# One sum on DVE and one multiply on PE for each statistic of the convolution branch's layer norm

## The reference

```
def layer_norm(x, g=None, b=None):
    mu = jnp.mean(x32, axis=-1, keepdims=True)
    var = jnp.mean(jnp.square(x32 - mu), axis=-1, keepdims=True)
    y = (x32 - mu) * lax.rsqrt(var + LN_EPS)
...
h_c = causal_dwconv(c_a * jax.nn.sigmoid(c_b), cf_w, cf_b)
y_c = jax.nn.silu(layer_norm(h_c, cf_ln_g, cf_ln_b)) * jax.nn.silu(c_g)
g_m = jax.nn.sigmoid(merge).reshape(bsz, slen, N_BRANCH, D_MODEL)
m = (g_m[:, :, 0] * (y_a @ w_branch[0])
     + g_m[:, :, 1] * (y_b @ w_branch[1])
     + g_m[:, :, 2] * (y_c @ w_branch[2]))
```

## Time and profile before

| | |
|---|---|
| median of 3 runs | 2294.22 us (2293.9 to 3189.31) |
| the profiled execution | 2294.44 us, span 2292.6 us |
| PE busy | 2214.4 us, 97% of the span |
| DVE busy | 1250.4 us, 55% |
| ACT busy | 779.0 us, 34% |
| mean granted TensorE clock | 0.986 |
| data moved | 217.93 MB, mean 95 GB/s |

### The profile page before, as it was taken

The page is one execution under the profiler, slowest core; times in us unless marked ns, Lnnn a source line. Parts: engine busy times, 40 slices in busy tenths (PEclk is TensorE's granted clock), DMA queues, the critical chain, the costliest instruction groups (busy, mean ns, idle before and its releaser), DMA issues.

```text
span 2292.6 us, 25818 instructions
## 1 busy us (share of the span) xinstructions
PE 2214.4 (97%) x10758; PEld 1822.4 (79%) x10770; DVE 1250.4 (55%) x1656; ACT 779.0 (34%) x1112; POOL 35.4 (2%) x46
## 2 busy tenths in 40 slices
PE   3999999999999799999999999999999999999998
PEld 2788888888788697877788888889787778888887
DVE  7798797933454836422745554224642375555422
ACT  1223232223343244344343333224434434333211
POOL 1000000000000110000000000000000000000000
PEclk7999999999999999999999999999999999999999
DMA  8332332332133222222123322213222222332221
GB/s 301 116 102 91 106 97 79 110 110 92 60 106 115 71 77 74 92 92 74 56 74 110 103 94 98 101 65 97 69 92 92 74 74 65 102 110 92 93 101 74
DMA packets 188242, 217.93 MB, mean 95 GB/s; under 512 B 3808, under 2 KB 167262, under 8 KB 188126
## 3 DMA queue, kind: packets, MB, share of 16 engines
q1 hardware_dynamic: 184128, 210.52, 27.7%
q10 hardware_dynamic: 3262, 3.60, 0.5%
q0 software_dynamic: 736, 2.15, 0.2%
HBM read 212.06 MB, written 4.19 MB: 94 GB/s over the span
## 4 chain that ended last, share of the span: by engine, by line
PE 91%; DVE 6%; ACT 1%; issue 1%; POOL 0%; DMA 0%; SPq 0%; ACTq 0%; POOLq 0%; DVEq 0%
PE psum L1582 28%; PE psum L1583 28%; PE psum L1584 28%; DVE whl L459 1%; PE psum L1807 1%; DVE adsum L1037 1%; PE psum L1796 1%; PE psum L1819 1%; PE psum L1878 1%; PE psum L1849 1%; PE psum L1860 1%; DMA x<-in_x 0%; DVE stat L1006 0%; PE psum L1906 0%; ACT whl L452 0%
## 5 line engine op out<-in xcount | busy, mean ns | idle before, releaser
L1582 PE MATMUL psum<-hT,whl 128*128 128x512 f32 (+1 forms) x2112 | 805.2, 381 | 8.5 <-DVE hT L1059 5.8
L1583 PE MATMUL psum<-hT,whl 128*128 128x512 f32 (+1 forms) x2112 | 797.3, 377 | 0.0
L1584 PE MATMUL psum<-hT,whl 128*128 128x512 f32 (+1 forms) x2112 | 797.2, 377 | 0.0
L459 DVE TENSOR_TENSOR whl<-raw,whl 128x1024 fp32r<-128x1024 f32 (+1 forms) x368 | 449.8, 1224 | 610.4 <-ACT whl L452 610.4
L452 ACT ACTIVATE whl<-raw 128x1024 fp32r<-128x1024 f32 (+1 forms) x368 | 384.4, 1048 | 478.0 <-PE psum L1584 441.3
L1582 PEld LDWEIGHTS psum<-hT,whl 128*128 128x128 f32 x2112 | 399.2, 189 | 90.9 <-DVE hT L1059 9.2
L1584 PEld LDWEIGHTS psum<-hT,whl 128*128 128x128 f32 x2112 | 399.2, 189 | 73.4
L1583 PEld LDWEIGHTS psum<-hT,whl 128*128 128x128 f32 x2112 | 399.5, 189 | 71.1 <-issue 0.7
L1582 PE MATMUL psum<-whl,ff 128*128 128x512 f32 x352 | 139.2, 396 | 2.2 <-DVE fsil L1561 2.2
L1584 PE MATMUL psum<-whl,ff 128*128 128x512 f32 x352 | 138.9, 395 | 0.0
L1583 PE MATMUL psum<-whl,ff 128*128 128x512 f32 x352 | 138.9, 395 | 0.0
(11 more groups left out here) (268 smaller groups left out, 2167.4 us busy)
## 6 DMA issues: line engine op xcount, KB each, us to landing
raw<-in_w_in SPq DMA_DIRECT2D x88, 1024.0 KB, 5.1
raw<-in_w_up SPq DMA_DIRECT2D x44, 1024.0 KB, 5.1
raw<-in_w_down SPq DMA_DIRECT2D x20, 1024.0 KB, 5.0
ada<-in_w_ada SPq DMA_DIRECT2D x12, 1024.0 KB, 10.1
raw<-in_w_branch SPq DMA_DIRECT2D x12, 1024.0 KB, 5.1
raw<-in_w_out SPq DMA_DIRECT2D x12, 1024.0 KB, 5.0
x<-in_x SPq DMA_DIRECT2D x4, 512.0 KB, 7.4
v_by_token<-vnat ACTq DMA_DIRECT2D x4, 512.0 KB, 2.8
```

Source lines behind the costliest of these rows:

```text
L459: nc.vector.tensor_tensor(whl_view(w, 1), raw_view(w), whl_view(w, 0).bitcast(F), ALU.subtract).then_inc(w_lo, 1)
L1582: M(out_, stat_hi, mov_hi, start=start, stop=False, **kw)
L1583: M(out_, stat_hi, mov_lo, start=False, stop=False, **kw)
L1584: return M(out_, stat_lo, mov_hi, start=False, stop=stop, **kw)
```

## The change

For the mean, DVE adds the eight tiles of `hc` in halves: four and four, two and two, one and one, into `sq` (three additions of 128x2048, 128x1024, 128x512), at m=1 of branch 1; PE multiplies the one tile that is left with `onesd`. For the variance, DVE adds the eight tiles of squares in the same way after column 3 of branch 1, and PE multiplies the one tile; this multiply now stands behind the two gate tiles of q=2, not ahead of them. DVE's epsilon, reciprocal and products move from m=5 of the gate loop to m=4 of the branch loop (behind the split for that tile), and ACT's root behind the gate of column 4. The first sum waits for PE's last tile of branch 0, because `sq` lies where that tile's operand was. The mean and the variance then differ from before only in the order of the additions.

```diff
@@ scalar @@
-                        if i == 1 and m == 5:
-                            act.wait_ge(ve, 1)
-                            A(sq[:, 0, :], sq[:, 0, :], ACT.Sqrt).then_inc(sqr, 1)
...
                             gate_tanh(("w_in", MG + 8 * i + m), mT[:, m, :] if i == 0 else tg[:])
+                            if i == 1 and m == 4:
+                                act.wait_ge(ve, 1)
+                                A(sq[:, 0, :], sq[:, 0, :], ACT.Sqrt).then_inc(sqr, 1)
@@ vector @@
+            def halved(a, b, n):
+                return V.tensor_tensor(sq[:, 0:n, :], a, b, ALU.add)
...
                         split_lo(W[("w_in", MG + 8 * i + m)] + 3)
+                        if i == 1 and m == 1:
+                            w_wait_full(dve, ("w_branch", 0, 7))
+                            dve.wait_ge(hc_done, KT)
+                            link(halved(hc[:, 0:4, :], hc[:, 4:8, :], 4))
+                            link(halved(sq[:, 0:2, :], sq[:, 2:4, :], 2))
+                            halved(sq[:, 0:1, :], sq[:, 1:2, :], 1).then_inc(hc_sum, 1)
...
-                        if i == 1 and m == 5:
-                            dve.wait_ge(var_ps, 1)
...
                         split_lo(W[key] + 3)
+                        if i == 1 and m == 4:
+                            dve.wait_ge(var_ps, 1)
...
                         V.tensor_tensor(mT[:, m, :], mT[:, m, :], g, ALU.add).then_inc(m_part, 1)
+                        if i == 1 and m == 3:
+                            dve.wait_ge(sqd, KT)
+                            link(halved(sq[:, 0:4, :], sq[:, 4:8, :], 4))
+                            link(halved(sq[:, 0:2, :], sq[:, 2:4, :], 2))
+                            halved(sq[:, 0:1, :], sq[:, 1:2, :], 1).then_inc(sq_sum, 1)
@@ tensor @@
                     if i == 1 and q == 1:
 
-                        pe.wait_ge(hc_done, KT)
+                        pe.wait_ge(hc_sum, 1)
                         take(STAT_BANK)
-                        for k in range(KT):
-                            ins = M(bank(STAT_BANK), onesd[:], hc[:, k, :], start=k == 0, stop=k == KT - 1)
-                        ins.then_inc(mean_ps, 1)
+                        M(bank(STAT_BANK), onesd[:], sq[:, 0, :], start=True, stop=True).then_inc(mean_ps, 1)
                         give(STAT_BANK, cen, KT)
-                    if i == 1 and q == 2:
-
-                        take(STAT_BANK)
-                        for k in range(KT):
-                            pe.wait_ge(sqd, k + 1)
-                            ins = M(bank(STAT_BANK), onesd[:], sq[:, k, :], start=k == 0, stop=k == KT - 1)
-                        ins.then_inc(var_ps, 1)
-                        give(STAT_BANK, ve, 1)
                     for j in range(2):
                         col_tile(("w_in", MG + 8 * i + 2 * q + j), h_at(0), h_at(1))
+                    if i == 1 and q == 2:
+
+                        pe.wait_ge(sq_sum, 1)
+                        take(STAT_BANK)
+                        M(bank(STAT_BANK), onesd[:], sq[:, 0, :], start=True, stop=True).then_inc(var_ps, 1)
+                        give(STAT_BANK, ve, 1)
```

More of the change, by code:

```diff
@@ L372, in build @@
         sp_hi, sp_lo = sem("sp_hi"), sem("sp_lo")
+        hc_sum, sq_sum = sem("hc_summed"), sem("squares_summed")
         rope_done, z_ps, sb_abs, sb_l, sp_ready, e_ps, sb_attn, sbo_ps, ob_hi, ob_lo = (
@@ L1227, in _ @@
                                 V.tensor_tensor(hc[:, k, :], hc[:, k, :], bank(STAT_BANK), ALU.subtract).then_inc(cen, 1)
-                        if i == 1 and m == 5:
-                            dve.wait_ge(var_ps, 1)
[L1230 to L1233, removed]
-                            for k in range(KT):
-                                V.tensor_tensor(hc[:, k, :], hc[:, k, :], sq[:, 0, :], ALU.mult).then_inc(nrm, 1)
                         if i == 1 and m == 7:
@@ L1246, in _ @@
                         split_lo(W[key] + 3)
+                        if i == 1 and m == 4:
+                            dve.wait_ge(var_ps, 1)
+                            V.tensor_scalar(sq[:, 0, :], bank(STAT_BANK), LN_EPS, None, ALU.add).then_inc(ve, 1)
+                            dve.wait_ge(sqr, 1)
+                            link(V.reciprocal(sq[:, 0, :], sq[:, 0, :]))
+                            dve.wait_ge(cen, KT)
+                            for k in range(KT):
+                                V.tensor_tensor(hc[:, k, :], hc[:, k, :], sq[:, 0, :], ALU.mult).then_inc(nrm, 1)
                         w_wait_full(dve, key)
```

## The result

The changed kernel takes 2284.14 us (median of 5 runs, 2281.51 to 2286.76). The ratio to the kernel before is 0.9947, with a 95% interval of 0.9937 to 0.9958: some 12 us or 0.5% less, with 9.7 to 14.5 us inside the interval. The 2294.22 us of the kernel before would give only 10.1 us. That is the median of three runs, and it lies low: 25 runs of the same kernel, taken beside the experiments, have a median of 2296.29 us (2293.77 to 2299.56), 12.15 above 2284.14. The forecast was 2282.2, the range 2278.5 to 2287.

A forecast was written before the change was run, and what follows sets the result against it. The prediction took PE's work to bound the kernel, with DVE's added work hidden: 2294.22 us less 12.02 us (14 instructions x 0.429 us, twice) gives 2282.2 us, range 2278.5 to 2287.

The forecast's parts named there:

- PE bounds the kernel: Between 580 and 764 us PE is busy without a hole, so each microsecond of PE work removed is gained.
- 12.02 us for 28 instructions at 0.429: At both statistics groups, PE drops 14 of 16 instructions at 0.429 us each: 6.01 us less, twice.
- what is left of a group: PE's two remaining instructions per statistic: 0.46 us taken; at full pitch 0.86 us, making the gain 11.2 us.
- A chain of 4.3 us: DVE's three halving additions per statistic: 2.29 + 1.22 + 0.69 + 0.08 = 4.3 us (3.2 to 4.8), off PE's path.
- the straight line's 2.29: DVE's untraced 128x2048 addition, extended in a line from the two smaller sizes: 2286 ns, taken as 2290.
- 9.2 and 5.1 forecast: Time to spare between DVE's chain and PE's multiply: 9.2 us at the mean, 5.1 us at the variance.
- The rest of the norm: Reciprocal and products end at 619.7, 7.5 us earlier while PE is 12 us earlier: 4.5 us of lead used up.
- the conversion behind the low parts: DVE's conversion for branch 2's second gate tile ends at 643.0, needed at 646.9: lead falls from 5.9 to 3.9 us.
- the sum: The prediction's reckoning of times and leads; its total was 2294.22 - 12.02 = 2282.2 us.
- the clock's play: Slow-clock stretches behind the change may begin or end elsewhere: 3 us either way, nothing in the sum.
- The rival on the slow side: PE waits for the sum of squares and the clock falls: slower above 7.5 us of wait, say 2296.7 us; chance 0.02.
- the fall at 800 us: Clock at 0.50 after a 9.6 us wait at the change of stage: half of 9.0, 4.5 us lost.

The follow-up runs named there:

- e4: Changed kernel with two more 128x2048 additions on DVE ahead of the sum of squares: 2284.22 us, ratio to the kernel before 0.9951.
- e5: Changed kernel with six more 128x2048 additions on DVE ahead of the sum of squares: 2294.15 us, ratio to the kernel before 0.9996.
- the kernels with fillers: Constant multiplies put in PE's wait at the first change of stage; on the changed kernel 2283.37 to 2284.91 us, on the kernel before (eight multiplies) ratio 1.0002.
- the one with 11 and 2: Changed kernel with eleven constant multiplies in PE's wait at the first change of stage and two behind the transposes: 2283.37 us, ratio to before 0.9941.
- e1: Kernel before with only the mean changed (three DVE additions, one PE multiply), the variance as before: 2289.89 us, ratio 0.9971.
- e2: Changed kernel with the mean's eight PE multiplies put back, so only the variance is changed: 2290.18 us, ratio to before 0.9973.
- e0: The changed kernel run again, code unchanged: 2284.26 us, ratio to the kernel before 0.9949.
- e3: Changed kernel with PE multiplying each DVE sum eight times over, for both statistics: 2296.63 us, ratio to the kernel before 1.0004.
- e6: Changed kernel with the variance's one multiply ahead of the two gate tiles of its group, not behind: 2291.56 us, ratio to before 0.9983.

## Why the prediction was right

**PE bounds the kernel.** Right. Four kernels with PE's instructions taken away or put back follow them to 0.05 us in the interval (213.08, 207.15, 207.13, 201.16).

**12.02 us for 28 instructions at 0.429.** Right in the place where they stand: 11.97. The choice between 0.46 and 0.86 us for what is left of a group fell on the right side (0.45 and 0.46).

**A chain of 4.3 us, hidden.** Right: 4.27 us for the variance's, with 2.28 for the size that the trace did not show, between the bounds of 1.22 and 2.76 and near the straight line's 2.29. Leads of 9.4 and 5.1 us were measured, 9.2 and 5.1 forecast, and `e4` and `e5` enclose the second: 4.6 us more cost nothing, 13.9 cost 8.8 of wait.

**The rest of the norm uses up lead.** Right: the products ended at 619.1 (619.7 forecast) and the conversion behind the low parts at 642.1 (643.0), 0.6 and 0.9 us earlier, as the whole program was 0.7 earlier at the first group. The lead of that conversion was 4.4 us, where the sum had 3.9. No wait came of it.

**The time itself.** 2284.14 is 1.9 us above the forecast, and the gain has no part in that: by medians it is 12.0 (2296.29 and 2284.26), where the sum had 12.02. What was off is the number that the gain was taken from. 2294.22 was the median of three runs, 2.1 us below that of 25, so the forecast of the time came out as much too low. The range was wide enough for it.

**The scatter, and the clock's play.** From the matmuls of the attention statistics in the second layer to the last matmul the profiles fall into two kinds. It is 457.3 us before, 457.7 and 457.1 in the two halves of the change, 457.2 with two more additions, 457.3 with the multiply first; but 459.9 and 459.6 in the two profiles of the changed kernel, 460.4 with sixteen multiplies on PE, 460.0 with six more additions. (Of the kernels with fillers three are of the first kind and the one with 11 and 2 of the second, 459.7.) The kernel with sixteen multiplies is as long as that of before, and the one with two more additions is the changed kernel to within a hidden chain, so this step of some 2.6 us doesn't go with the gain. The first kind waits 2.5 us for DVE at the second layer's `w_out_2`, the second 4.0 to 4.1. In all eight profiles of the first kind the granted clock is 0.50 from 14 to 12 us before that wait ends and 1.00 behind it; in all five of the second it is 1.00 there, and between 0.50 and 0.68 in the 4 us behind it. So a slow stretch lies ahead of a wait for DVE, which then becomes 1.5 us shorter, or behind it, where nothing takes it up; that this makes the step is a reading of the profiles, and no run tests it. The first layer has a like step, of 2.5 or 4.0 us of wait, and the two layers have it independently of each other: the profile of before has neither, that of the changed kernel the second layer's only, `e1`, `e2` and `e4` have the first layer's only, `e0` and `e3` both. What sets it in one execution and not in another is open. The allowance of 3 us either way was about right: the runs of the changed kernel scatter over 5 us.

**The rival on the slow side.** Its mechanism exists and `e5` and `e6` show it: a wait, and the clock's fall behind it. Its price was too high. I had taken 4.5 us from the fall at 800 us, as half of 9.0; but the row has PE busy for 7.50 of the 9.00 us, half of which is 3.75, and the part of that in the transposes only shortens a wait for POOL. The fillers show 2.2 us there, and behind the variance it is 2.8 and 3.0. So the change would lose its gain at some 9 us of wait, not 7.5, and `e5`, with 8.8, lies at that point: its ratio is 0.9996. That an idle TensorE goes back to the lower clock, as the Trainium skill says (TensorE: Matmul & The Clock Gate, section "HAM oscillation"), the stretches of both agree with: 0.50 behind a wait of 5.7 us too.

## What to carry to other kernels

Where PE is busy without a hole, count its instructions and read their pitch from the starts (here the weight loads), not from the durations: 28 x 0.429 us gave the gain to a twentieth of a microsecond, where the durations of 592 ns would have said 16.6. Work moved to an idler engine is free only while its hand-over keeps a lead; work the lead out tile by tile, and put the consumer behind other ready work, since here two tiles' distance was worth 7.3 us by the medians and 8.7 in the interval. The two waits made here, of 5.7 and 8.8 us, cost their length and then some 3 us of halved clock, so a lead of a few microseconds is worth more than it seems. Before a small difference is put down to an edit, or a forecast is built on a time, look how far executions of one kernel lie apart: three runs put the base of this forecast 2 us too low, a sixth of the gain.

## What the runs showed of the hardware

- An fp32 multiply of 128x512 is two instructions with a pitch of 0.429 us each, as against 0.23 us for one of the three passes of a split product. Behind such a group the next tile's first step is 0.63 to 0.64 us, whether the group has 2 instructions or 16.
- Behind a wait of 5.7 us (`e6`) or 8.8 us (`e5`) the granted clock was 0.50 for some 5 to 6 us of work, at a price of 3.0 and 2.8 us, nearly the same for both lengths. Behind the waits of 2.5 us at the second layer's `w_out_2` it was 1.00 in all eight profiles that have them.
- At the first change of stage PE works for some 7.5 us at half the clock, and a held clock would give back 2.2 us there: the part in the transposes only shortens a wait for POOL (1.50 us, and 2.37 when the transposes run faster).
- Executions of one kernel lie up to 5.8 us apart (2293.8 to 2299.6) with nothing changed. The profiles show a step in each layer that is there or not, of some 2.6 us in the second and 1.5 to 2.4 us in the first, with a wait of 4.0 in place of 2.5 us; a difference of 3 us so needs many runs, or an interval inside the profile, which repeats to 0.01 us (201.16 in two executions of the changed kernel and in that of `e4`, 201.15 or 201.16 in those with fillers).
